# Hybrid-mixer encoder layer on one core: sparse-attention pairs one round behind the local blocks, pooling's scaling on VectorE, pooled products behind the gate turns

## The chip, the cores and the metric

The kernel runs on one core of a Trainium2 chip. The metric is the device time of one execution in microseconds (us), as the median of several runs. Engines are named as in the profile: PE (TensorE; PEld is its weight load), DVE (VectorE), ACT (ScalarE), POOL (GpSimd) and SP (SyncE, which only issues transfers here).

## The reference

One layer of a streaming encoder, 1024 positions by 1024 channels, float32. An adaLN-conditioned RMSNorm feeds one input projection, whose columns go to four token mixers of 256 channels each; their outputs are normalised, concatenated and projected; a gated MLP with a causal depthwise convolution follows, and a final norm.

```python
ya = gmlp_mixer(za, ws, bs)            # spatial gating over blocks of 128 positions
yb = dsa_mixer(q, k, v, qi, ki, wi)    # top-256 keys of a ReLU indexer, then softmax attention
yc = pool_mixer(zc, w, scale)          # below
yd = swa_mixer(q, k, v, sinks)         # window of 128 positions with sinks
x = x + g1 * (rms(concat(ya, yb, yc, yd)) * mix_out_g @ w_out)
x = x + g2 * conv_glu(h, w_up, conv_w, conv_b, w_down)
```

The pooling mixer: for each of four groups of 64 channels with window 2, 4, 8 or 16, the trailing sum of the window over `min(count, window)`, minus the input itself, times a 64x64 matrix per group, times a scale per channel. The change touches how it is computed and when, and the order of the two attentions.

## The kernel before, in words

Positions are split in 8 blocks of 128 (NBLK) and two halves of 4 blocks (HB). Every large product is exact to float32 by splitting each operand in a high and a low part: three matmuls of 128x512 for each 128x128 weight tile. ACT makes the high part of a weight unit (`hi`), POOL the low part (`lo`, line 584), DVE helps at the start. Each engine works through its own list in order and waits on semaphores; the lists are written out by hand and nothing reorders them.

**Input units.** 19 units of 128 columns (N_IN) are projected one after another; ACT moves each out of PSUM (`evac`). Beside them PE computes the indexer's products (`dot`), ACT their ReLU, DVE sums them to scores (`accumulate`). DVE then finds the keys of blocks 2 and 3 by rounds of maximum and replace (`early_round`, lines 1476 and 1482), 32 rounds in all, and starts a bisection for blocks 4 to 7 (`search`, a generator whose pieces `search_for(us)` takes until their nominal lengths fill the budget; each trial counts keys, line 1387). POOL multiplies the adaLN weights by the condition (`ada_products`, line 615), ACT sums them (`ada_sums`).

**Pooling.** Units 9 and 10 (U_C) are the pooling input `zc[0]`, `zc[1]`, each 128 channels of two windows. POOL builds the window sums in `win_a` and `win_b` by doubling (`doubled`, line 591): for `zc[0]` behind unit 14, for `zc[1]` behind units 17 and 18. ACT scales them by one over the window (`pool_scale`, line 826), for `zc[1]` only after all eight gate evacuations. POOL then corrects the first 16 positions (line 597) and subtracts the input (`pool_out`, line 598), and signals `pool_ready`. PE multiplies by the pooling weights in two halves of four blocks (`pooled`, line 2048), into banks 0 and 1 both times, and DVE scales the results into `y` (`pool_outputs`, line 1564).

**The mixers.** After the last input unit PE transposes the gating input block by block (`gate_turn`, line 2004), ACT copies it out (`gate_inputs`, line 938). Then a loop over k interleaves, on PE, DVE and ACT, the local (window) attention of block k with the pairs of sparse-attention heads of the first half. There are 8 pairs (PAIRS), two heads each, two pairs to a block, and pair d runs in round k = d + BEHIND with BEHIND = 2, so the loop has NBLK + BEHIND + 1 = 11 rounds, the first of which has no earlier work to carry and the last ones only sparse work. In round k:

- PE: `swa_values(k-1)` (line 2034), `swa_turn(k, 0)`, `values(d-1, 1)`, `turn(d, 0)`, `swa_turn(k, 1)`, `logits(d+2)` (line 2087), `turn(d, 1)`, `swa_logits(k+2)` (line 2013), `values(d, 0)`; in rounds 0 and 1 also `pooled(k)`.
- DVE: `swa_softmax(k+1)` (lines 1542 to 1548), `soft(k+1-BEHIND)` (line 1612), `swa_out(k-1)`, and spread over the rounds the gMLP statistics (`ln_mean` line 1527, `ln_var` line 1532), the masks of blocks 2 and 3 (`mask_of`, line 1490), `early_out`, the adaLN values (line 1716, round 3), `gmlp_scale` (round 6) and `gmlp_output` (round 8).
- ACT: the exponentials and copies of both attentions.
- POOL: centring and squaring of the gMLP input (lines 686, 689), then the low part of unit 20, then the sum of bias and mask (`masked_bias`, line 670) that `soft(4)` to `soft(7)` need.

Then PE turns `y` (line 2169, 64 small matmuls), and the output projection and the MLP follow with PE always busy. DVE goes on with the bisection beside them: `columns_beside_search` takes pieces between output columns. Its result is needed when the second half's sparse attention starts.

```python
def link(eng, s, ins):       # vlink on DVE, plink on POOL
    ins.then_inc(s, 1)
    eng.wait_ge(s, chain[s.name])
```

## Time and profile before

| what | value |
| --- | --- |
| median of 3 runs | 1263.75 us (1262.98 to 1265.56) |
| the profiled execution's own time | 1264.89 us |
| its span | 1262.9 us |
| PE busy | 1210.7 us, 96% |
| DVE busy | 716.9 us, 57% |
| ACT busy | 580.1 us, 46% |
| POOL busy | 615.1 us, 49% |
| share of PE in the chain that ended last | 86% |
| mean granted clock of PE | 0.985 |

The chain of waits is the way back from the last instruction, at each step to what released it. An engine can be busy all along and yet not be on it. The windows view gives the busy time of each engine in a stretch; a timeline row gives the start of a group of equal instructions, their busy time together and, in brackets, how long the engine had been idle and who ended that. "issue" there is time without a visible reason. Between about 365 us and the end PE is busy without a break but for a few joints, so what matters for the change lies before.

### The profile page before, as it was taken

What the parts mean: (1) busy time and instruction counts of PE and PEld (TensorE: products, weight loads), DVE (VectorE), ACT (ScalarE), POOL (GpSimd) and SP (SyncE); (2) the same over time, 40 slices, a digit from 0 to 9 for tenths busy, and PEclk for the clock granted to TensorE, in tenths of its full rate; (3) what the DMA queues carried; (4) which work ended last, traced back from release to release, by engine and by line L of the source; (5) the groups of instructions that cost most, each with busy time, mean ns of one, the idle gap of its engine ahead of it and who ended that gap; (6) DMA issues with size and microseconds to landing.
All of it is one profiled execution on the core that took longest, in us unless ns stands there. A gap on an engine that the chain in (4) does not pass through costs nothing.

```text
span 1262.9 us, 17256 instructions
## 1 busy us (share of the span) xinstructions
PE 1210.7 (96%) x5814; PEld 1003.5 (79%) x5814; DVE 716.9 (57%) x1412; ACT 580.1 (46%) x997; POOL 615.1 (49%) x309
## 2 busy tenths in 40 slices
PE   6898999987899999999999999999999999999997
PEld 5687788866788888888888887888888888888876
DVE  5953777896968798999983334353522211121233
ACT  5245566645843444134423666552544134422443
POOL 0045756783414255445545666434355445544555
PEclk8899999997999999999999999999999999999999
DMA  8557563450122122232224442424222222222223
GB/s 309 190 186 262 173 204 107 171 150 18 51 84 104 63 100 99 89 112 100 100 100 142 134 142 103 164 76 155 70 100 100 99 87 97 100 100 100 88 106 139
DMA packets 58665, 153.93 MB, mean 122 GB/s; under 512 B 6600, under 2 KB 20296, under 8 KB 58608
## 3 DMA queue, kind: packets, MB, share of 16 engines
q1 hardware_dynamic: 47760, 135.64, 31.2%
q10 hardware_dynamic: 10848, 17.57, 4.3%
q8 instruction: 31, 0.51, 0.2%
q14 instruction: 26, 0.21, 0.1%
HBM read 142.66 MB, written 10.52 MB: 121 GB/s over the span
## 4 chain that ended last, share of the span: by engine, by line
PE 86%; DVE 4%; ACT 4%; DMA 2%; POOL 2%; issue 1%; ACTq 0%; SPq 0%; DVEq 0%; POOLq 0%
PE ps L1938 24%; PE ps L1941 24%; PE ps L1939 24%; PE ps L2229 2%; PE ps L1917 1%; DMA x_sb<-in_x 1%; PE ps L1918 1%; PE ps L1962 1%; PE ps L2218 1%; PE ps L2208 1%; PE ps L1922 1%; PE ps L1864 1%; POOL w_ada L615 1%; PE ps L2242 1%; DMA qi_dram<-qi_lo 1%
## 5 line engine op out<-in xcount | busy, mean ns | idle before, releaser
L575 POOL TENSOR_TENSOR w_lo<-w_raw,w_hi 128x1024 fp32r<-128x1024 f32 x148 | 354.8, 2398 | 436.9 <-ACT w_hi L757 436.9
L1938 PE MATMUL ps<-h_hi,w_hi 128*128 128x512 f32 x896 | 355.4, 397 | 2.6 <-POOL w_lo L584 2.6
L1939 PE MATMUL ps<-h_lo,w_hi 128*128 128x512 f32 x896 | 350.4, 391 | 0.0
L1941 PE MATMUL ps<-h_hi,w_lo 128*128 128x512 f32 x896 | 331.7, 391 | 0.0
L757 ACT ACTIVATE w_hi<-w_raw 128x1024 fp32r<-128x1024 f32 x148 | 156.8, 1059 | 329.6 <-PE ps L1941 322.3
L1938 PEld LDWEIGHTS ps<-h_hi,w_hi 128*128 128x128 f32 x896 | 168.9, 189 | 37.6 <-POOL w_lo L584 3.4
L1941 PEld LDWEIGHTS ps<-h_hi,w_lo 128*128 128x128 f32 x896 | 168.5, 188 | 35.9
L1939 PEld LDWEIGHTS ps<-h_lo,w_hi 128*128 128x128 f32 x896 | 169.2, 189 | 32.7
L1797 DVE SCALAR_TENSOR_TENSOR ps<-conv_in,conv_w,ps 128x512 f32<-128x512 f32 x44 | 33.2, 754 | 205.4 <-ACT ps L1170 205.4
L1938 PE MATMUL ps<-act_hi,w_hi 128*128 128x512 f32 x352 | 139.7, 397 | 2.2 <-DVE act_lo L1738 2.2
L1941 PE MATMUL ps<-act_hi,w_lo 128*128 128x512 f32 x352 | 137.4, 390 | 0.0
L1939 PE MATMUL ps<-act_lo,w_hi 128*128 128x512 f32 x352 | 137.2, 390 | 0.0
L1387 DVE TENSOR_SCALAR_CACHE_REDUCE unread<-score,trial 128x640 uint8<-128x640 f32 (+1 forms) x124 | 130.2, 1076 | 2.2
L1744 DVE SCALAR_TENSOR_TENSOR x<-ps,mod,x 128x512 f32<-128x512 f32 (+1 forms) x64 | 48.0, 749 | 135.8 <-PE ps L1941 135.7
L615 POOL TENSOR_TENSOR w_ada<-w_ada,cond 128x1024 f32<-128x1024 f32 x32 | 76.6, 2405 | 45.5 <-DMA w_ada<-in_w_ada 45.3
L1938 PEld LDWEIGHTS ps<-act_hi,w_hi 128*128 128x128 f32 x352 | 66.2, 188 | 15.9 <-DVE act_lo L1738 2.8
L1941 PEld LDWEIGHTS ps<-act_hi,w_lo 128*128 128x128 f32 x352 | 66.1, 188 | 14.0
L1939 PEld LDWEIGHTS ps<-act_lo,w_hi 128*128 128x128 f32 x352 | 66.2, 188 | 12.7
L1370 DVE SCALAR_TENSOR_TENSOR score<-ps,wis,score 128x512 f32<-128x512 f32 (+3 forms) x70 | 46.0, 657 | 29.3 <-ACT ps L817 25.7
L1177 ACT ACTIVATE conv_t<-ps 128x512 f32<-128x512 f32 x44 | 26.3, 598 | 70.6 <-DVE ps L1801 70.5
L817 ACT ACTIVATE ps<-ps 128x512 f32<-128x512 f32 (+3 forms) x80 | 38.8, 501 | 33.9 <-PE ps L1962 33.8
L1938 PE MATMUL ps<-y_hi,w_hi 128*128 128x512 f32 x128 | 50.1, 392 | 0.0
(264 smaller groups left out, 1856.7 us busy)
## 6 DMA issues: line engine op xcount, KB each, us to landing
w_raw<-in_w SPq DMA_DIRECT2D x173, 512.0 KB, 3.2
w_ada<-in_w_ada SPq DMA_DIRECT2D x48, 512.0 KB, 4.3
x_sb<-in_x SPq DMA_DIRECT2D x4, 1024.0 KB, 9.6
q_st<-qk_dram SPq DMA_DIRECT2D x32, 128.0 KB, 4.3
out<-fin_o ACTq DMA_DIRECT2D x14, 256.0 KB, 2.1
qi_st<-qi_dram ACTq DMA_DIRECT2D x18, 128.0 KB, 4.5
qk_dram<-qk_hi ACTq DMA_DIRECT2D x4, 512.0 KB, 2.7
qk_dram<-qk_lo ACTq DMA_DIRECT2D x4, 512.0 KB, 3.7
```

Source lines behind the costliest of these rows:

```text
L575: pool.tensor_tensor(r(w_lo[:, slot]), w_raw[:, slot], w_hi[:, slot], ALU.subtract).then_inc(w_lo_ready, 1)
L615: pool.tensor_tensor(t, t, cond[:], ALU.mult).then_inc(ada_weighted, 1)
L757: act.activation(r(w_hi[:, slot]), w_raw[:, slot], ACT.Copy).then_inc(w_hi_ready, 1)
L817: act.activation(ps[:, 4 + i % 4, 0:n], ps[:, 4 + i % 4, 0:n], ACT.Relu, scale=IDX_DIM ** -0.5).then_inc(relu_ready, 1)
L1177: act.activation(conv_t[:, u], ps[:, u], ACT.Gelu_apprx_tanh).then_inc(gelu_ready, 1)
L1370: dve.scalar_tensor_tensor(out=dst, in0=ps[:, 4 + i % 4, 0:n], scalar=wgt, in1=dst, op0=ALU.mult, op1=ALU.add).then_inc(scores_added, 1)
L1387: dve.tensor_scalar(unread[:, b % 2, 0:P * (b + 1)], sc_of(b), limit, None, op, ALU.add, accum_out=found[:, b - HB:b - HB + 1]).then_inc(k ...
L1744: dve.scalar_tensor_tensor(out=o, in0=ps[:, bank], scalar=gate, in1=o, op0=ALU.mult, op1=ALU.add).then_inc(residual_added, 1)
L1797: dve.scalar_tensor_tensor(out=ps[:, u], in0=conv_in[:, u, 1:HALF + 1], scalar=conv_w[:, w_row, 1:2], in1=ps[:, u], op0=ALU.mult, op1=ALU. ...
L1938: pe.matmul(ps[:, bank], r(hi_t[:, kk]), r(xh(kk)), start=(i == 0), stop=False)
L1939: pe.matmul(ps[:, bank], r(hi_t[:, kk]), r(xl(kk)), start=False, stop=False)
L1941: mm = pe.matmul(ps[:, bank], r(lo_t[:, kk]), r(xh(kk)), start=False, stop=last_k)
```

## The change

- `BEHIND` is 1: pair d runs in round d + 1, and the loop has 10 rounds. `logits(0)` is issued ahead of the loop. `ada_sums(18)` on ACT goes from round 1 to round 0.
- Pooling: `pool_scale` on ACT and `pool_out` on POOL go away. DVE does both in `pool_mix`: two instructions for each window, one for the first 16 positions and one that scales and subtracts. `pool_mix(0)` stands behind the first 25 top-8 rounds, `pool_mix(1)` behind the two masks, which come ahead of the mixers too.
- The bisection gets 6.0 in place of 9.0 twice before the mixers, and 4.2 in place of 3.6 beside the MLP's columns.
- PE's pooled products of block b come directly behind `gate_turn(b)`, the second half in banks 6 and 7. The first of them waits for both `pool_mix`. DVE's `pool_outputs`, second half first, both come in round 0 behind all the means, and `swa_turn(0, 0)`, which writes bank 6, waits for the first.

```diff
-        BEHIND = 2
+        BEHIND = 1
...
+        POOL_BANKS = ((0, 1), (6, 7))
...
                 elif n == U_POOL + 2:
-                    pool.wait_ge(pool_scaled, 2)
-                    pool_out(0, 0, win_a)
-                    pool_out(0, 64, win_b)
-                elif n == U_POOL + 3:
+                    pool.wait_ge(pool_mixed, 2)
                     doubled(zc[1], 1, win_a, 0)
                     doubled(win_a, 2, win_b, 0)
-                elif n == U_POOL + 4:
+                elif n == U_POOL + 3:
                     doubled(win_b, 4, win_a, 0)
                     doubled(win_a, 8, win_b, 64)
                     pool.sem_inc(pool_summed, 1)
             ada_products(N_IN - 1)
-            pool.wait_ge(pool_scaled, 4)
-            pool_out(1, 0, win_a)
-            pool_out(1, 64, win_b)
-            pool.sem_inc(pool_ready, 1)
...
             gate_inputs(6)
             gate_inputs(7)
-            act.wait_ge(pool_summed, 2)
-            pool_scale(0, win_a, 8)
-            pool_scale(64, win_b, 16)
...
-                        if k == 1:
+                        if k == 0:
                             ada_sums(N_IN - 1)
...
+            def pool_mix(tile, wins):
+
+                dve.wait_ge(pool_summed, tile + 1)
+                for row, sums, win in zip((0, 64), (win_a, win_b), wins):
+                    rows = slice(row, row + 64)
+                    vlink(dve.scalar_tensor_tensor(out=sums[rows, 16:32], in0=sums[rows, 16:32], scalar=float(win),
+                                                   in1=pool_c[rows, tile], op0=ALU.mult, op1=ALU.mult))
+                    dve.scalar_tensor_tensor(out=zc[tile][rows, 16:], in0=sums[rows, 16:], scalar=1.0 / win,
+                                             in1=zc[tile][rows, 16:], op0=ALU.mult, op1=ALU.subtract).then_inc(pool_mixed, 1)
...
+                if step == DOT_STEPS:
+                    pool_mix(0, (2, 4))
                 if taken == ROUNDS and step + 1 < TOP_STEPS:
-                    search_for(9.0)
+                    search_for(6.0)
+            dve.wait_ge(top8_marked, ROUNDS + DROP_ROUNDS)
+            for b in EARLY:
+                mask_of(b)
+            dve.sem_inc(masks_ready, 1)
+            pool_mix(1, (8, 16))
...
                         if k == 0:
-                            ln_mean(2)
-                            ln_mean(3)
-                        if k == 1:
+                            for b in range(2, NBLK):
+                                ln_mean(b)
+                            pool_outputs(1)
                             pool_outputs(0)
...
-                        columns_beside_search(nd, 5 * KD, 0, 3.6)
+                        columns_beside_search(nd, 5 * KD, 0, 4.2)
...
+                if (b, j) == (0, 0):
+                    pe.wait_ge(pool_out_ready, 1)
...
             for b in range(NBLK):
                 gate_turn(b)
+                pooled(b)
...
                 if h == 0:
+                    logits(0)
                     for k in range(NBLK + BEHIND + 1):
...
-                        if k < 2:
-                            pooled(k)
```

PE's list from the first gate turn on, before (za_t is the gating input, dk and dq the local attention's keys and queries, zc the pooling input):

```order
L2004 MATMUL ps<-ident,za_t 128x128 [waits unit_out]
L2004 MATMUL ps<-ident,za_t 128x128 x7
L2004 MATMUL ps<-ident,za_t 128x128 [waits gm_out]
L2004 MATMUL ps<-ident,za_t 128x128 x3
L2004 MATMUL ps<-ident,za_t 128x128 [waits gm_out]
L2004 MATMUL ps<-ident,za_t 128x128 x3
L2013 MATMUL ps<-dk,dq 128x256 [waits swa_biased]
L2013 MATMUL ps<-dk,dq 128x256 x3
L2004 MATMUL ps<-ident,za_t 128x128 [waits gm_out]
```

and with the change, where the product of block 0 stands between the turns of blocks 0 and 1, with a wait of its own:

```order
L1986 MATMUL ps<-ident,za_t 128x128 [waits unit_out]
L1986 MATMUL ps<-ident,za_t 128x128 x3
L2029 MATMUL ps<-pool_w,zc_97 128x128 [waits pool_w_loaded,pool_mixed]
L2029 MATMUL ps<-pool_w,zc_98 128x128
L1986 MATMUL ps<-ident,za_t 128x128 x4
L2029 MATMUL ps<-pool_w,zc_97 128x128
L2029 MATMUL ps<-pool_w,zc_98 128x128
L1986 MATMUL ps<-ident,za_t 128x128 [waits gm_out]
L1986 MATMUL ps<-ident,za_t 128x128 x3
L2029 MATMUL ps<-pool_w,zc_97 128x128
```

Seven turns have moved behind that wait.

DVE's list at the end of the input units, before (score and unread belong to the bisection, swa_bias to the local attention):

```order
L1413 TENSOR_SCALAR trial<-ps 128x2 [waits bound_ready]
L1387 TENSOR_SCALAR unread_126,ps<-score,trial 128x640 [waits trial_set]
L1513 TENSOR_SCALAR kept<-ps 128x8 [waits keys_counted]
L1515 MEMSET swa_bias_in 128x4x64 [waits swa_table_loaded,dve_chain]
L1516 MEMSET swa_bias_in 64x4x64 [waits dve_chain]
L1517 MEMSET swa_bias_in 64x4x64 [waits dve_chain]
L1519 COPY swa_bias<-swa_bias_in 128x1024 [waits unit_done,dve_chain]
L1542 COPY logit<-sinks 128x4 [waits swa_logits_ready,dve_chain]
L1543 SCALAR_TENSOR_TENSOR logit<-ps,swa_bias 128x4x128
```

and with the change, from the third and last trial on:

```order
L1396 TENSOR_TENSOR ps<-ps,wanted 128x2 [waits keys_counted]
L1398 COPY_PREDICATED ps<-ps,trial 128x2 [waits trial_judged]
L1465 TENSOR_SCALAR score<-score 128x384 [waits top8_marked]
L1465 TENSOR_SCALAR score<-score 128x512 [waits dve_chain]
L1472 SCALAR_TENSOR_TENSOR win_a<-win_a,pool_c 64x16 [waits dve_chain,pool_summed]
L1474 SCALAR_TENSOR_TENSOR zc_98<-win_a,zc_98 64x1024 [waits dve_chain]
L1472 SCALAR_TENSOR_TENSOR win_b<-win_b,pool_c 64x16
L1474 SCALAR_TENSOR_TENSOR zc_98<-win_b,zc_98 64x1024 [waits dve_chain]
L1505 TENSOR_SCALAR kept<-ps 128x8 [waits keys_counted]
L1507 MEMSET swa_bias_in 128x4x64 [waits swa_table_loaded,dve_chain]
L1508 MEMSET swa_bias_in 64x4x64 [waits dve_chain]
L1509 MEMSET swa_bias_in 64x4x64 [waits dve_chain]
L1511 COPY swa_bias<-swa_bias_in 128x1024 [waits unit_done,dve_chain]
```

Two masks and the four instructions of `pool_mix(1)` now stand between the bisection and the local attention's table.

DVE's list behind the third pair of `ln_var`, round 3, before (mod and scale_g are the adaLN values, logit_69 the sparse attention's logits, bias its unmasked table, bias_e POOL's sum of bias and mask):

```order
L1716 TENSOR_TENSOR mod<-ada,b_ada 128x32 [waits ada_rest_summed]
L1717 TENSOR_SCALAR scale_g<-mod 128x8 [waits dve_chain]
L1718 TENSOR_TENSOR scale_g<-scale_g,norm_g 128x8 [waits dve_chain]
L1542 COPY logit<-sinks 128x4 [waits swa_turned,swa_logits_ready]
L1543 SCALAR_TENSOR_TENSOR logit<-ps,swa_bias 128x4x256
L1547 TENSOR_REDUCE sm_max_s<-logit 128x4 [waits swa_biased]
L1548 TENSOR_SCALAR sm_neg_s<-sm_max_s 128x4 [waits dve_chain]
L1612 SCALAR_TENSOR_TENSOR logit_69<-ps,bias_68 128x256 [waits dsa_turned,dsa_logits_ready] x2
L1620 TENSOR_REDUCE sm_max<-logit_69 128x1 [waits dsa_biased]
```

and with the change:

```order
L1698 TENSOR_TENSOR mod<-ada,b_ada 128x32 [waits ada_rest_summed]
L1699 TENSOR_SCALAR scale_g<-mod 128x8 [waits dve_chain]
L1700 TENSOR_TENSOR scale_g<-scale_g,norm_g 128x8 [waits dve_chain]
L1534 COPY logit<-sinks 128x4 [waits swa_turned,swa_logits_ready]
L1535 SCALAR_TENSOR_TENSOR logit<-ps,swa_bias 128x4x256
L1539 TENSOR_REDUCE sm_max_s<-logit 128x4 [waits swa_biased]
L1540 TENSOR_SCALAR sm_neg_s<-sm_max_s 128x4 [waits dve_chain]
L1603 SCALAR_TENSOR_TENSOR logit_69<-ps,bias_e 128x384 [waits bias_and_mask,dsa_turned,dsa_logits_ready] x2
L1611 TENSOR_REDUCE sm_max<-logit_69 128x1 [waits dsa_biased]
```

The first pair that needs POOL's `bias_e` follows these `ln_var` one round sooner.

## Rows read from the trace of the kernel before

**Rows 1.** The windows view of the opening (busy us and instructions by engine, clock, DMA share).
```profile
285.00:290.00 5.00, 3.42 (x14) 2.44 (x14) 1.40 (x4) 2.77 (x11) 4.65 (x4) 0.50 0.00 0
```

**Rows 2.** PE's timeline: start us, busy us, group [idle before <-releaser].
```profile
286.93 2.08 PE L2013 MATMUL ps<-dk,dq 64*128 64x256 f32 x8
...
293.88 1.00 PE L2034 MATMUL ps<-dv,swa_pt 128*128 128x64 f32 x8
...
300.01 1.90 PE L2034 MATMUL ps<-dv,swa_pt 128*128 128x64 f32 x16
...
311.02 1.95 PE L2034 MATMUL ps<-dv,swa_pt 128*128 128x64 f32 x16
...
316.90 1.95 PE L2034 MATMUL ps<-dv,swa_pt 128*128 128x64 f32 x16
...
323.19 1.13 PE L2013 MATMUL ps<-dk,dq 64*128 64x256 f32 x8
...
324.75 1.95 PE L2034 MATMUL ps<-dv,swa_pt 128*128 128x64 f32 x16
...
346.83 1.90 PE L2034 MATMUL ps<-dv,swa_pt 128*128 128x64 f32 x16
...
358.12 7.36 PE L2169 MATMUL ps<-diag_y,y 128*128 128x128 f32 x64
```

**Rows 3.** The chain that ended last, in the opening: start us, us, what.
```profile
283.05 0.67 ACT win_a L826
...
285.41 2.36 POOL zc L598
288.14 2.35 POOL zc L598
```

**Rows 4.** DVE's timeline from the last top-8 rounds to the first pooled outputs.
```profile
227.45 0.69 DVE L1476 MAX8 top<-score 128x8 f32<-128x512 f32 x1
...
248.80 0.69 DVE L1476 MAX8 top<-score 128x8 f32<-128x512 f32 x1
...
256.70 0.16 DVE L1413 TENSOR_SCALAR trial<-ps 128x2 int32<-128x2 int32 x1
...
259.21 0.16 DVE L1413 TENSOR_SCALAR trial<-ps 128x2 int32<-128x2 int32 x1
...
270.45 0.17 DVE L1513 TENSOR_SCALAR kept<-ps 128x8 int32<-128x8 int32 x1
...
272.67 2.22 DVE L1519 COPY swa_bias<-swa_bias_in 128x1024 f32<-128x1024 f32 x1 [0.90 <-PE ps L1941]
...
278.47 0.97 DVE L1548 TENSOR_SCALAR sm_neg_s<-sm_max_s 128x4 f32<-128x4 f32 x1
279.35 0.41 DVE L1527 TENSOR_REDUCE st<-gm 128x4 f32<-128x256 f32 x1
...
294.08 1.29 DVE L1564 TENSOR_TENSOR y<-ps,pool_s 128x512 f32<-128x512 f32 x2 [0.84 <-PE ps L2048]
```

**Rows 5.** The source view of lines 1738 and 1282: ns min/median/max, first and last start.
```profile
L1738 DVE TENSOR_TENSOR act_lo<-act_f,act_hi x6: 2275/2381/2397, 506.0 to 1217.9; 128x512 fp32r<-128x512 f32 x6
...
L1282 DVE SCALAR_TENSOR_TENSOR h_t<-x_sb,scale_g,rms_x x8: 1283/1285/1289, 27.7 to 69.9; 128x1024 f32<-128x1024 f32 x8
```

**Rows 6.** POOL's timeline.
```profile
240.83 2.41 POOL L584 TENSOR_TENSOR w_lo<-w_raw,w_hi 128x1024 fp32r<-128x1024 f32 x1
...
316.37 0.61 POOL L686 TENSOR_TENSOR vn<-gm,st 128x256 f32<-128x256 f32 x1 [4.64 <-DVE st L1532]
...
321.25 1.96 POOL L670 TENSOR_TENSOR bias_e<-bias,score 128x384 f32<-128x384 f32 x2
```

**Rows 7.** DVE's timeline in rounds 3 to 5.
```profile
316.47 0.56 DVE L1716 TENSOR_TENSOR mod<-ada,b_ada 128x32 f32<-128x32 f32 x1
...
321.23 0.74 DVE L1612 SCALAR_TENSOR_TENSOR logit<-ps,bias 128x256 f32<-128x256 f32 x2
...
327.34 1.02 DVE L1612 SCALAR_TENSOR_TENSOR logit<-ps,bias_e 128x384 f32<-128x384 f32 x2
```

More of the change, by code:

```diff
@@ L592, in doubled @@
                                          src[row:P, win - 1:16 + S - win], ALU.add))
-            def pool_out(tile, row, sums):
-                rows = slice(row, row + 64)
-                plink(pool.tensor_tensor(sums[rows, 16:32], sums[rows, 16:32], pool_c[rows, tile], ALU.mult))
-                plink(pool.tensor_tensor(zc[tile][rows, 16:], sums[rows, 16:], zc[tile][rows, 16:], ALU.subtract))
             pool.memset(eps[:], EPS).then_inc(consts_set, 1)
@@ L821, in relus @@
                     stack_queries(b + 2)
-            def pool_scale(row, sums, win):
-                rows = slice(row, row + 64)
-                act.activation(sums[rows, 32:], sums[rows, 32:], ACT.Copy, scale=1.0 / win).then_inc(pool_scaled, 1)
             def v_evac(g):
@@ L1587, in _ @@
             ln_mean(1)
-            dve.wait_ge(top8_marked, ROUNDS + DROP_ROUNDS)
             for h in range(2):
@@ L1699, in _ @@
                             swa_out(k - 1)
-                        if k == 1:
-                            pool_outputs(1)
-                        if k >= BEHIND + 2 and k % 2 == 0:
+                        if k >= BEHIND + 2 and (k - BEHIND) % 2 == 0:
                             early_out((k - BEHIND - 2) // 2)
-                        if k < 2:
-                            ln_mean(2 * k + 4)
-                            ln_mean(2 * k + 5)
                         if 1 <= k < 5:
@@ L2037, in swa_values, with pooled @@
                 mm.then_inc(swa_product, 1)
[L2039 to L2041 removed]
+            def pooled(b):
+                if b == 0:
+                    pe.wait_ge(pool_mixed, 4)
                     pe.wait_ge(pool_w_loaded, 16)
[L2043 to L2050 removed]
+                for t in range(2):
+                    at_ = W * (b % 2) + P * t
+                    mm = pe.matmul(ps[:, POOL_BANKS[b // HB][(b // 2) % 2], at_:at_ + P],
+                                   zc[t][:, 16 + P * b:16 + P * b + P], pool_w[:, t], start=True, stop=True)
+                if b % HB == HB - 1:
+                    mm.then_inc(pool_done, 1)
             pe.wait_ge(unit_out, N_IN - 1)
```

27 lines of the change are left out of this document (3 added, 24 removed).

## The prediction

> **What bounds the kernel now.** I read the chain first: PE holds 86% of it, so only PE's idle stretches and its slow ones can be won. The windows put those in one place, between the last input unit (273 us) and the turning of `y` (358.12 us, [rows 2]). In the opening PE works 3.42 of 5 us at half clock, granted 0.50, that is 1.2 in place of 2.4 GHz [rows 1]. Twice as long shows in PE's timeline: eight products of `swa_logits` take 2.08 us there and 1.13 us later [rows 2].
>
> PE's timeline then gives the mixer's rounds by the start of `swa_values`: round 1 at 293.88, round 2 at 300.01, round 3 at 311.02, round 4 at 316.90, round 5 at 324.75, round 8 at 346.83, the turns at 358.12 [rows 2]. So rounds 1 and 2 cost 17.1 us, 3 and 4 13.7 us, 5 to 7 22.1 us, the last three 11.3 us. The chain shows what holds the opening: ACT's two scalings from 283.05, POOL's two subtractions (2.36 and 2.35 us, from 285.41 and 288.14), then PE's pooled products [rows 3].
>
> A third thing is to be seen in DVE's timeline: some short instructions are long. The table copy `swa_bias` takes 2.22 us and `sm_neg_s` on four numbers 0.97 us [rows 4]; in both cases POOL is in the middle of an instruction and DVE ends just after it. `act_lo` = `act_f` - `act_hi`, both inputs in SBUF, 512 elements, takes 2.38 us in the median, each time beside a POOL instruction of 2.4 us [rows 5].
>
> **Part 1, the opening.** It decides the sign of a large term, so it is followed in time.
>
> *pool_mix(0).* The top-8 rounds start at 227.45 and 14 of them take up to 248.80, 1.525 us each [rows 4]. The eighth ends at 239.65. Bare, pool_mix(0) is two large instructions of 1024 elements at 1.28 us (line 1282, two SBUF inputs, [rows 5]) and two of 16 elements, estimated at 0.2: 3.0 us. But POOL runs an adaLN product until 240.83 and `lo` for 2.41 us behind it [rows 6]. By `act_lo` [rows 5] DVE waits out both: 1.2 + 2.4 us. I take 6.5 us, to 246.1. The bounds are 3.0, if such an instruction does not wait, and 9.0 with a third wait.
>
> The Trainium skill (SBUF — State Buffer, Who interferes with whom) says that a VectorE instruction with two SBUF inputs contends with a GpSimd instruction that reads SBUF. By that rule the change puts eight such instructions among POOL's, and the sum is the one below. The trace agrees for `act_lo`; no row shows `scalar_tensor_tensor` on 64 partitions beside POOL.
>
> *Bisection, masks, pool_mix(1).* Seven rounds more end at 256.8. The bisection's first trial came 6.5 us after the rounds and I take 4.3 us, since POOL now waits for a transfer there; then three trials of 2.51 us (256.70 to 259.21, [rows 4]) in place of five and a half: 268.7. The masks are estimated at 0.5 us each, plus a wait of 1.0 and one of 2.4 behind POOL: 273.1. pool_mix(1) with 3.0 us and a wait of 2.4: 278.4. If the order with POOL falls out otherwise, the bisection ends up to 4 us later, but by then POOL has no work left to wait for, so the end moves little.
>
> *First softmax.* Before, `kept` ran at 270.45, and `swa_bias` could start only with the last unit, 272.67 [rows 4]. Now `kept` starts at 278.4, memsets and copy take 2.0, the first softmax 1.7: `sm_neg_s` ends at 282.1, against 279.44 (278.47 + 0.97, [rows 4]). PE waits for `pool_mix` from about 274.5 to 278.4, and the seven gate turns queue behind that.
>
> *To round 1.* DVE: two means, the second softmax 2.7, six means, at 0.53 each (0.41 and a short one behind it, [rows 4]): 289.0. `pool_outputs(1)` 1.3 [rows 4]: 290.3. Only then may `swa_turn(0, 0)` write bank 6. `pool_outputs(0)` and `soft(0)`'s first part give 292.3, `logits(1)` and `swa_logits(2)` 2.7 us at a clock between the levels [rows 2]: round 1 starts at 295.0, against 293.88. **Loss 1.1 us.** ACT's 2.1 us and POOL's 4.9 us of `pool_scale` and `pool_out` are gone from the chain [rows 3], but DVE's lateness and the seven means in one piece eat them. Without any wait for POOL, this is a gain of 3.7.
>
> **Part 2, rounds 1 and 2.** Before, DVE in round 1 waited for each half of the products, and with it the masks and four means stood between; that is why round 2 took 11.0 us. All of it has moved ahead. Round 3 took 5.9 us [rows 2] with larger pairs. I take 5.4 and 5.5: 10.9 in place of 17.1. **Gain 6.2 us**; bounds 3 (a round of 7 us, as rounds 5 to 7 have) and 7.
>
> **Part 3, rounds 3 and 4.** The pairs are one round sooner, the rest stays. POOL's path does not shorten: from the third `ln_var` pair at 316.4, `vn` for two blocks, `lo` of unit 20 and two sums of bias, to 323.2 (321.25 + 1.96, [rows 6]), 6.8 us. DVE's path does: before, it used them at 327.34, 10.9 us after `mod` began at 316.47 [rows 7]. Now `soft(4)` stands where `soft(3)` stood at 321.23 [rows 7], 4.8 us after, of which 0.9 is a wait for POOL; 3.9 without it. **A new wait** of some 2.3 us on DVE, in which PE stands in front of `logits(5)`, loses its clock and pays about 1.4 us more on what follows (2.08 for 1.13 us, [rows 2]). Rounds 3 and 4 take 17.5 in place of 13.7: **loss 3.8 us**; bounds 0 (POOL in time) and 6.
>
> **Part 4, rounds 5 to 7.** DVE, ACT and PE each have about the same list, the table loads for the gMLP root included: 22.1 us stay 22.1. Here the distances logits, softmax, exponential, turn are the same with `BEHIND` 1 as with 2, so no wait comes from it.
>
> **Part 5, the end.** The tail has lost a round. From round 8's start: PE 1.8 `swa_values`, four pieces of 0.9 for gating and values, two turns 0.9, values of the last two heads 0.9, so 7.2 us; then `early_out` and the reciprocal and first diagonal on DVE, 1.6: 8.8 in place of 11.3. **Gain 2.5 us**; bounds 1 and 3.5.
>
> **Part 6, the search moved behind.** Some 6 us of trials run beside the MLP now. The budget of 4.2 gives DVE the same three pieces per column as 3.6 for the later blocks. The cover is PE's work of over 300 us there, and the search now ends many columns before its result is used. I cost it at nothing; if a column's update came late, PE would lose at most a piece, 1.3 us.
>
> **The sum.** -1.1 + 6.2 - 3.8 + 0 + 2.5 = 3.8 us, rounded to 4. The profiled execution took 1264.9 us (span 1262.9 us), 1.1 above the median of 1263.75; I take the difference off the median: **1259.8 us**.
>
> **Rivals.**
> 1. *No waiting on POOL's port.* If the new instructions run beside POOL at 3.0 us a `pool_mix`, the opening gains 3.7 in place of losing 1.1: gain 8.8, **1255.0 us**. Against it stands `act_lo`; for it, that POOL waits for its transfers in part of the time. If part 3's new wait fails to come too: 12.5, 1251.2.
> 2. *PE's queue behind the first pooled product.* `pooled(0)` waits for `pool_mix(1)`, with seven gate turns, the second local logits and so DVE's means behind it. My slack is negative already. Each further POOL instruction waited out costs 2.4 us on all that follows; from the second on, with part 2 at its low bound, the gain of 4 is gone: 4.0 - 4.8 - 1.5 = -2.3, **1266.0 us**, slower. It decides if pool_mix(1) ends after about 282 us.
> 3. *The rounds are bound by work, not by order.* Then one round fewer gives nothing at the end and rounds 1 and 2 give 3: 4.0 - 3.2 - 2.5 = -1.7, with part 3's loss at half again about zero: **1263.6 us**, no change.
>
> The Trainium skill (Perfetto Trace Analysis, Optimizing Scalar/DVE Operations) advises the other way than this change: where VectorE is saturated, work may go to ScalarE. Only the second rival would follow from it, as DVE is the engine that PE waits for at 278 us; the chance given to it already counts that.
>
> **How the numbers follow.** My sum 0.44, rival 1 0.24, rival 2 0.15, rival 3 0.17. A measurement of this kernel tells about 0.2%, 2.5 us, from no change. The sum's own bounds let a little of its chance fall within that. So: faster 0.70, same 0.16, slower 0.14. The range takes rival 1 and most of rival 3 and the edge of rival 2: 1253.5 to 1264.5.
>
> **What would show it.** `pool_mix(0)` beginning at about 239.7 and lasting over 6 us; large `zc` instructions on DVE of 2 to 3.6 us; `pool_mix(1)` ending near 278; the first `swa_values` near 295, rounds 1 and 2 of 5.4 us; DVE idle before the first `bias_e` instruction, released by POOL; 8.8 us from round 8's `swa_values` to the first turn of `y`, near 354. Wrong if `zc` instructions take 1.3 us (rival 1), if the first `swa_values` comes after 299 (rival 2), or if rounds 1 and 2 take over 14 us (rival 3).

## The result

The changed kernel is slower: 1274.18 us median of 20 executions (1263.64 to 1277.38), against 1265.44 us for the kernel before on the same chips; ratio 1.0047, 95% interval 1.0029 to 1.0065 (the two medians alone would give 1.0069, as more than half of the new times lie in an upper group). The forecast was 1259.8 us, faster; both its sign and its range (1253.5 to 1264.5) were wrong.

The executions of the changed kernel differ more than those of the kernel before, and they differ by TensorE's mean granted clock. Eight of the 20 took 1263.6 to 1266.5 us at a mean clock of 0.980 to 0.985, twelve 1271.4 to 1277.4 us at 0.971 to 0.978. The profiled one (1275.1 us, span 1273.1 us, clock 0.972) is of the upper kind; that of the kernel before (1264.9 us, span 1262.9 us) had 0.985. So the trace shows where the time is in the slower executions, and the experiments have to show which part is always there. No execution of the lower kind was profiled for this kernel.

**The profile after.** The windows from the opening to round 7 (busy us and instructions of PE, PE's weight loads, DVE, ACT, POOL; then clock, DMA share, GB/s):

```profile
270.00:280.00 10.00, 5.89 (x34) 5.11 (x33) 9.20 (x17) 2.43 (x4) 2.19 (x1) 0.71 0.83 207
280.00:290.00 10.00, 7.26 (x55) 6.34 (x54) 7.78 (x23) 5.86 (x15) 2.42 (x4) 0.95 0.01 3
290.00:300.00 10.00, 8.41 (x36) 6.53 (x37) 7.26 (x23) 7.40 (x25) 0.00 (x0) 0.56 0.19 55
300.00:310.00 10.00, 9.76 (x44) 8.36 (x44) 5.73 (x15) 4.42 (x17) 3.98 (x7) 0.50 0.00 1
320.00:330.00 10.00, 6.53 (x36) 4.83 (x35) 6.68 (x13) 5.82 (x20) 6.97 (x7) 0.77 0.16 52
330.00:340.00 10.00, 10.00 (x48) 9.30 (x50) 5.90 (x14) 4.36 (x14) 2.50 (x2) 0.55 0.00 0
```

PE's timeline, with its idle stretches in brackets (L2018 is `swa_values`, the start of a round):

```profile
275.97 1.22 PE L2029 MATMUL ps<-pool_w,zc 128*128 128x128 f32 x4 [3.64 <-DVE zc L1474]
...
290.08 0.41 PE L2008 MATMUL ps<-ident,logit 128*128 128x128 f32 x2 [2.54 <-DVE y L1556]
...
295.03 1.97 PE L2018 MATMUL ps<-dv,swa_pt 128*128 128x64 f32 x8
303.25 3.62 PE L2018 MATMUL ps<-dv,swa_pt 128*128 128x64 f32 x16
312.45 1.95 PE L2018 MATMUL ps<-dv,swa_pt 128*128 128x64 f32 x16
...
325.88 1.65 PE L2070 MATMUL ps<-k_st,q_st 128*128 128x384 f32 x4 [3.31 <-DVE logit L1603]
330.80 3.62 PE L2018 MATMUL ps<-dv,swa_pt 128*128 128x64 f32 x16
...
355.97 1.89 PE L2018 MATMUL ps<-dv,swa_pt 128*128 128x64 f32 x16
...
365.30 9.01 PE L2151 MATMUL ps<-diag_y,y 128*128 128x128 f32 x64 [2.04 <-DVE diag_y L1658]
```

Two things differ from [rows 2]. The waits are longer (3.64, 2.54, 3.31 and 2.04 us), and behind them PE works at 1.2 GHz: `swa_values` of sixteen products takes 3.62 us in rounds 2 and 5 and 1.95 in the others, the turns of `y` 9.01 in place of 7.36. In the windows PE is busy 9.76 of 10 us at 0.50 and 10.00 of 10 at 0.55: there it is no longer waiting, it is slow.

The same steps side by side, from starts in PE's timeline, with three kernels of the experiments below ("two behind" is the change without its one round behind):

| us | before | forecast | after | two behind | after, waits filled | after, POOL's order |
|---|---|---|---|---|---|---|
| first `swa_values` | 293.88 | 295.0 | 295.03 | 295.17 | 294.98 | 296.38 |
| rounds 1, 2 | 17.1 | 10.9 | 17.4 | 13.6 | 14.3 | 13.4 |
| rounds 3, 4 | 13.7 | 17.5 | 18.4 | 13.7 | 16.5 | 14.2 |
| rounds 5 to 7 | 22.1 | 22.1 | 25.2 | 22.1 | 23.2 | 22.2 |
| round 8 to turns of `y` | 11.3 | 8.8 | 9.3 | 11.3 | 9.2 | 9.3 |
| turns to first product of the output projection | 7.1 | not priced | 8.8 | 7.1 | 7.2 | 7.1 |
| from there to the end | 897.7 | as before | 899.0 | 897.5 | 899.1 | 897.6 |

Before to after, the differences are +1.15, +0.3, +4.6, +3.1, -2.0, +1.7 and +1.4: together the 10.2 us between the two spans. Of these the first is no larger than chance: a second profile of the changed kernel, below, has its first `swa_values` at 296.17, 1.1 us after this one.

DVE's timeline holds what the prediction said of the port (`pool_mix(0)`, then `pool_mix(1)`):

```profile
237.53 1.18 DVE L1472 SCALAR_TENSOR_TENSOR win_a<-win_a,pool_c 64x16 f32<-64x16 f32 x1
238.74 1.22 DVE L1474 SCALAR_TENSOR_TENSOR zc<-win_a,zc 64x1024 f32<-64x1024 f32 x1
239.99 2.27 DVE L1472 SCALAR_TENSOR_TENSOR win_b<-win_b,pool_c 64x16 f32<-64x16 f32 x1
242.29 1.22 DVE L1474 SCALAR_TENSOR_TENSOR zc<-win_b,zc 64x1024 f32<-64x1024 f32 x1
...
273.03 0.17 DVE L1472 SCALAR_TENSOR_TENSOR win_a<-win_a,pool_c 64x16 f32<-64x16 f32 x1 [0.16 <-DVE score L1465]
273.24 1.22 DVE L1474 SCALAR_TENSOR_TENSOR zc<-win_a,zc 64x1024 f32<-64x1024 f32 x1
...
279.55 0.17 DVE L1540 TENSOR_SCALAR sm_neg_s<-sm_max_s 128x4 f32<-128x4 f32 x1
```

A 16-element instruction takes 1.18 or 2.27 us where POOL is at work and 0.17 where it is not. Which instruction carries the wait is a matter of the moment. In the second profile of the same program the first large one took it:

```profile
240.17 3.38 DVE L1474 SCALAR_TENSOR_TENSOR zc<-win_a,zc 64x1024 f32<-64x1024 f32 x1
243.58 0.17 DVE L1472 SCALAR_TENSOR_TENSOR win_b<-win_b,pool_c 64x16 f32<-64x16 f32 x1
```

There POOL's `lo` had begun at 240.07, 0.10 us ahead of DVE, and took its usual 2.40 us; so it is, with 3.37 to 3.46 us, in ten of the twelve profiles of kernels with this `pool_mix`. In the first profile DVE began 0.09 us ahead of `lo` and took 1.22 us, and POOL's `lo` took 3.39. The new wait of part 3 is there too, in DVE's and in POOL's timeline:

```profile
324.31 0.56 DVE L1603 SCALAR_TENSOR_TENSOR logit<-ps,bias_e 128x384 f32<-128x384 f32 x1 [1.06 <-POOL bias_e L657]
325.27 0.56 DVE L1603 SCALAR_TENSOR_TENSOR logit<-ps,bias_e 128x384 f32<-128x384 f32 x1 [0.40 <-POOL bias_e L657]
```
```profile
320.87 2.36 POOL L584 TENSOR_TENSOR w_lo<-w_raw,w_hi 128x1024 fp32r<-128x1024 f32 x1
323.18 3.87 POOL L657 TENSOR_TENSOR bias_e<-bias,score 128x384 f32<-128x384 f32 x4
```

### The profile page after: what moved, and what is told of

It reads as the page before. It is cut to its first block, busy times and chain, and to the rows that moved or that the text cites. A ratio compares the mean times of both kernels' runs of the same rounds, so it can differ in the third digit from the quotient of the medians.

```text
span 1273.1 us, 17248 instructions
## 1 busy us (share of the span) xinstructions
PE 1227.2 (96%) x5814; PEld 1019.0 (80%) x5814; DVE 723.1 (57%) x1420; ACT 577.1 (45%) x993; POOL 606.3 (48%) x301
## 4 chain that ended last, share of the span: by engine, by line
PE 82%; DVE 7%; DMA 3%; ACT 3%; POOL 2%; issue 2%; SPq 1%; ACTq 0%; DVEq 0%; POOLq 0%
PE ps L1920 22%; PE ps L1921 22%; PE ps L1923 22%; PE ps L2211 2%; DMA w_ada<-in_w_ada 1%; PE ps L2018 1%; PE ps L1899 1%; PE ps L1900 1%; PE ps L1944 1%; PE ps L2200 1%; PE ps L2190 1%; DVE score L1457 1%; PE ps L1995 1%; PE ps L1904 1%; PE ps L1846 1%
```

## The experiments

Theories: **clock** (behind new idle stretches PE's work runs at half clock, in some executions), **lateness** (the rounds wait for DVE, in all executions) and **order** (one round behind asks for `bias_e` before POOL has it). All times are medians. The experiments ran in four sets, each on a chip of its own, with the kernel before timed beside each (1264.1 to 1265.4 us); across sets the ratios to it are compared.

### The same kernel again, and its waits filled

> The changed kernel once more, unedited, beside the three edits of this call. Clock theory (TensorE's granted clock stays at half speed behind the new idle stretches, in some executions and not in others, and this is the whole loss): again times in two groups, 1263 to 1267 and 1271 to 1278 us, the upper group with a mean granted clock of 0.971 to 0.978, the lower with 0.980 or more. Rival lateness (VectorE is later on the path to the rounds, always, by the port waits and the queue behind the first pooled product): times spread evenly about 1270, not by clock.

Measured: 1268.47 us, 12 executions from 1263.38 to 1276.64. Five lie at 1274.7 to 1276.6 (clock 0.972 to 0.975), five at 1263.4 to 1266.4 (0.982 to 0.985), two between, at 1268.1 and 1268.9 (0.979): spread along the clock rather than in two clean groups. Another profile of the upper kind repeats the waits of the first to a hundredth (3.63, 2.54, 3.31 and 2.05 us, 9.01 for the turns of `y`), though the whole lies about 1.1 us later. With the first 20, 17 of 32 executions have a clock under 0.979; of the kernel before it is 15 of 114. At a clock of 0.982 to 0.985 the changed kernel takes 1264.9 us (12 executions) and the kernel before 1264.8 (63): **at the same clock they are equally fast.** (The mean clock is itself a result of the order, so this tells where the time is, and not what made the clock fall.)

```
+            def hold(count, at_):
+                for _ in range(count):
+                    pe.matmul(at_, ident[:], ident[:], start=True, stop=True)
...
+                if (b, j) == (0, 0):
+                    pe.wait_ge(swa_biased, 2)
+                    hold(16, ps[:, 2, 0:P])
...
+                    hold(26, ps[:, 0, 0:P])
                     pe.wait_ge(pool_mixed, 4)
...
+                    if i == 5:
+                        hold(24, ps[:, 0, 2 * P:3 * P])
```

> The changed kernel with matmuls that nobody reads issued by TensorE where it stood idle: 26 before its wait for pool_mixed, 16 before swa_turn(0, 0), 24 before logits(5). Nothing else moves, and VectorE's instructions stay where they were. Clock theory: granted clock 0.9 to 1.0 from 280 to 340 us, rounds 1 and 2 take 14 us or less in place of 17.4, rounds 5 to 7 22 in place of 25.2, and all executions lie in one group, 1259 to 1266 us. Rival lateness: the rounds wait for VectorE, so a higher clock gives nothing; 1264 to 1277 as without them. Rival order (one round behind makes POOL's bias_e late): the same as rival lateness.

Measured: 1268.2 us (1264.68 to 1271.62), clock 0.982 to 0.988, none of 12 under 0.979; of the unfilled kernel, in the same set, it was five of 12. PE's timeline:

```profile
274.44 5.97 PE L1875 MATMUL ps<-ident 128*128 128x128 f32 x52
...
289.17 3.79 PE L1875 MATMUL ps<-ident 128*128 128x128 f32 x32
...
319.38 5.52 PE L1875 MATMUL ps<-ident 128*128 128x128 f32 x48
```

The clock was 1.00 from 270 to 300 us and 0.83, 1.00, 1.00, 1.00 in the windows behind; the upper group is gone. But each filling matmul leaves two records, so they outlast the waits of 3.64, 2.54 and 3.31 us, and the 1259 to 1266 us expected were missed: the median is that of the unfilled kernel. With 13, 9, 12 and, before the turns of `y`, 8:

> The changed kernel with matmuls that nobody reads, this time no longer than the idle stretches that they fill (in the run with 26, 16 and 24 they took 5.97, 3.79 and 5.52 us, and the waits were 3.64, 2.54 and 3.31): 13 before pooled(0), 9 before swa_turn(0, 0), 12 before logits(5), 8 before the turns of y. Clock theory: granted clock near 1.0 from 276 to 375 us, first swa_values at 295 as in the changed kernel, rounds 1 and 2 13.8 us in place of 17.4, rounds 3 and 4 16 to 17.5, rounds 5 to 7 22, the turns of y 7.4 in place of 9.0; 1261 to 1265 us with a clock of 0.985 or more, and no execution over 1270. Rival: the rounds wait for VectorE and the clock is a companion, not a cause; then the median stays at 1268 to 1274.

Measured: 1265.96 us, 1257.39 to 1270.9, ratio to before 0.9999 (0.9977 to 1.0022). The four fastest (1257.4 to 1261.2) have clocks of 0.987 to 0.991, the rest 0.978 to 0.983; one of 12 is under 0.979, against 17 of 32 without filling. Two lie over the 1270 expected as the limit, and the median over the 1261 to 1265. Filling is work of its own: at 0.982 to 0.985 these kernels take 1269.6 us (six executions, long filling) and 1266.6 (seven, short), over the 1264.9 without. A count by clock flatters them, then; by time it is two of 12 over 1270 us, against 17 of 32. The medians part less clearly: the interval of this ratio overlaps that of the unfilled kernel's second run (1.0026, 1.0 to 1.0053). The profiled one (span 1264.4 us) has DVE's work where the changed kernel has it, the first `swa_values` at 294.98, and is 8.7 us shorter. So the lateness theory falls as an account of the loss, while the expected narrow group did not come: the clock still fell from 290 to 300 us (0.67).

### One round behind alone, and the rest alone

```
-        BEHIND = 2
+        BEHIND = 1
...
-                        if k < 2:
-                            pooled(k)
+                        if k == 0:
+                            pooled(0)
+                            pooled(1)
```

> The kernel before with the pairs one round behind alone (both pooled products and their outputs in round 0); pooling's scaling stays on ScalarE and GpSimd. Prediction's terms: part 5 gains 2.5, part 3 loses 3.8 with a wait of some 2 us on VectorE for bias_e, rounds 1 and 2 gain little as the products' waits remain in them: 1264 to 1269. Clock theory: slower than before only in executions in which the granted clock falls behind the wait of logits(5), by some 3 us. Rival order: 1268 or more in every execution, since the order alone is the loss.

Measured: 1278.38 us (6 executions, 1267.82 to 1285.41), ratio 1.0098 (1.0061 to 1.0134); clock 0.963 to 0.982, five of six under 0.979. DVE waits 1.06 and 0.40 us for `bias_e` here too. The 1264 to 1269 expected were missed, and the clock theory's 3 us of loss by far; the order rival's 1268 or more in every execution came but for one of 1267.8, the only one with a clock of 0.982. The run is not one round behind alone: both pooled products had to move into round 0, and in the profile the opening and rounds 1 and 2 are 5.7 us longer than before.

```
-        BEHIND = 1
+        BEHIND = 2
...
-                    logits(0)
```

> The changed kernel with the pairs two rounds behind again; pooling's scaling on VectorE and the pooled products behind the gate turns stay. Clock theory: the idle stretches of 3.6 and 2.5 us before pooled(0) and swa_turn(0, 0) stay, so does the low clock from 290 to 311 us in many executions, and the one before logits(5) goes: two groups, 1263 to 1266 and 1268 to 1274. Rival order: as fast as before or faster, 1260 to 1265, in one group. Rival lateness: 1266 to 1275 in one group.

Measured: 1262.37 us (1260.28 to 1268.44), ratio 0.9986 (0.9971 to 1.0); one of 12 under 0.979. The idle stretches of 3.65 and 3.45 us in the opening are there, and rounds 5 to 7 take 22.1 us. So the change's two halves have opposite signs: pooling on VectorE with the products behind the gate turns gives 3 us, though the interval reaches no gain, and one round behind costs 13 us without it (the moved products included) and 6 to 12 with it (1268.5 and 1274.2 against 1262.4). The clock theory expected a second group here and did not get it, the order rival's 1260 to 1265 came: these opening waits alone did not part the executions, though rounds 1 and 2 were slow in the first profile behind nearly the same ones. Joined, the two theories read: the order makes the wait in round 4, and the clock behind it makes it dear. That is tried next.

### POOL's order in round 3

```
-                    lo(N_IN + 1)
                     tables_ready(0)
...
                     for I in range(HEADS * 2, FIRST_LATE):
                         masked_bias(I)
+                        if I == HEADS * 2 + 1:
+                            lo(N_IN + 1)
```

> The changed kernel with GpSimd's lo of the input behind the first two sums of mask and bias and not ahead of them. Theory (with the pairs one round behind, VectorE needs bias_e 2.4 us before GpSimd has it, and TensorE loses 3.3 us before logits(5) and then its clock): VectorE's waits of 1.06 and 0.40 us for bias_e go, TensorE's wait before logits(5) falls to 1.5 us or less, rounds 3 and 4 take 15 to 16 us in place of 18.35, and round 5 7 in place of 10.4; median 1262 to 1268. Rival (the round is full of VectorE's own work at that place): the wait before logits(5) stays over 2.5 us, median as the changed kernel.

Measured: 1264.68 us (1259.8 to 1270.24), ratio to before 1.0 (0.9977 to 1.0023); three of 12 under 0.979. In the timelines of POOL, DVE and PE:

```profile
318.34 1.95 POOL L657 TENSOR_TENSOR bias_e<-bias,score 128x384 f32<-128x384 f32 x2
320.26 2.37 POOL L584 TENSOR_TENSOR w_lo<-w_raw,w_hi 128x1024 fp32r<-128x1024 f32 x1
```
```profile
320.24 1.01 DVE L1604 SCALAR_TENSOR_TENSOR logit<-ps,bias_e 128x384 f32<-128x384 f32 x2
```
```profile
321.30 0.97 PE L2071 MATMUL ps<-k_st,q_st 128*128 128x384 f32 x4 [1.36 <-DVE logit L1604]
...
355.55 7.38 PE L2152 MATMUL ps<-diag_y,y 128*128 128x128 f32 x64 [2.04 <-DVE diag_y L1659]
```

One POOL instruction moved behind two others: DVE does not wait, PE waits 1.36 us in place of 3.31, rounds 3 and 4 take 14.2 us in place of 18.4, and round 5 7.4 in place of 10.4. All came as expected or better; the rival (DVE full at that place) falls. Between the two profiles a wait that was 1.95 us longer goes with 7.1 us in rounds 3 to 7 (43.5 against 36.4). That is the price in these two executions and not a mean: this one is of the lower kind (1262.2 us), the other of the upper. How much kind matters is seen in rounds 1 and 2, which the edit does not touch: 13.4 us here and 17.4 there. And the turns of `y` ran at full clock behind the same wait of 2.04 us. By time two of 12 are over 1270 us here, as with filling, against 17 of 32 without the edit.

### The opening's order

```
+                            pool_outputs(1)
+                            pool_outputs(0)
                             for b in range(2, NBLK):
                                 ln_mean(b)
-                            pool_outputs(1)
-                            pool_outputs(0)
```

on the kernel two rounds behind:

> Two rounds behind as before, and in the opening VectorE's pool_outputs(1) and (0) ahead of the six ln_mean. Theory (TensorE's wait of 3.45 us before swa_turn(0, 0) is the queue of means on VectorE): the wait falls to 1.3 us, first swa_values at 293.0 in place of 295.17, 1260 to 1261. Rival (the means only move and are missed later, as softmax(2) or vn come late): first round's gain given back by round 3, 1262 to 1263.

Measured: 1263.8 us (1261.61 to 1265.16). PE's wait before `swa_turn(0, 0)` fell from 3.45 to 1.47 us and the first `swa_values` came at 291.99, 3.2 us sooner. Round 2 then took 9.9 us in place of 6.3 and the gain was gone. The reason is neither theory's:

```profile
300.00:310.00 10.00, 9.44 (x42) 7.93 (x42) 5.79 (x16) 4.25 (x16) 3.48 (x6) 0.50 0.14 40
```

PE was busy 9.44 of 10 us at 0.50, though its largest single wait since 289 us was 1.60 us. The median missed both forecasts.

With all eight gate turns ahead of the first pooled product as well:

```
             for b in range(NBLK):
                 gate_turn(b)
+            for b in range(NBLK):
                 pooled(b)
```

> The same and all eight gate turns ahead of the first pooled product. Theory (prediction's second rival: the gate turns, the second local logits and all behind them queue behind pooled(0), which waits for VectorE's pool_mix(1)): the idle stretch of 3.65 us before pooled(0) falls under 1.5, the last pooled product ends by 284 in place of 287.4, first swa_values at 291 to 292, 1257.5 to 1260. Rival (VectorE sets the opening, whatever TensorE's queue): first swa_values at 293 as with the outputs first alone, 1260 to 1262.

Measured: 1267.04 us (1260.52 to 1269.49), a miss for both; five of 12 under 0.979, so that two rounds behind do not by themselves hold the clock. The wait before `pooled(0)` went, and a longer one came. ACT's timeline, then PE's:

```profile
280.82 0.40 ACT L923 ACTIVATE logit<-logit,sm_neg_s 128x129 f32<-128x129 f32 x1 [3.52 <-DVE sm_neg_s L1540]
...
281.61 1.06 ACT L916 ACTIVATE gm<-ps 128x512 f32<-128x512 f32 x2
```
```profile
282.24 1.97 PE L1986 MATMUL ps<-ident,za_t 128*128 128x128 f32 x8 [5.52 <-ACT gm L916]
```

ACT empties the banks of the gate turns, and its exponentials of the first softmax stand in that queue: it waits 3.52 us for DVE's `sm_neg_s` with gate banks full behind it. The queue that matters is ACT's, not PE's.

Two rounds behind, with the pooled products back in rounds 0 and 1 (banks 0 and 1 for both halves, each half waiting for the other's outputs):

> Of the change only pooling's scaling on VectorE and the masks ahead of it: the pairs two rounds behind, the pooled products in rounds 0 and 1 again as in the kernel before, each half waiting for the outputs of the other. It parts the gain of 3.5 us that rounds 1 and 2 show with the products behind the gate turns (13.6 us in place of 17.1). Theory (that gain is the products' place): rounds 1 and 2 take 16 to 17.5 us again, first swa_values at 293 or earlier, since TensorE's four 3.64 and 3.45 us waits shrink, and the median is 1263.5 to 1266. Rival (the gain is the masks' and means' place, which this kernel keeps): rounds 1 and 2 under 15 us, median 1260 to 1263.

Measured: 1265.93 us (1261.59 to 1273.18). The first `swa_values` comes at 288.45, rounds 1 and 2 take 17.1 us again. So the 3.5 us of those rounds are the products' place, as the theory had it, and in the profiles they are more than paid for by an opening that is 6.7 us later (288.45 against 295.17). This kernel lost that lead in round 3, which ran at half clock behind a wait of 2.93 us and took 9.7 us in place of 5.9; three of its 12 executions are under 0.979.

### The best of each order, with filled waits

Two rounds behind, outputs first, 11 filling matmuls before `pooled(0)`, 4 before `swa_turn(0, 0)` and 6 before `swa_turn(1, 1)`:

> The kernel with two rounds behind and the outputs first, with matmuls that nobody reads in TensorE's waits: 11 before pooled(0), 4 before swa_turn(0, 0), 6 before swa_turn(1, 1). Clock theory (the 3.2 us that the outputs first gained were lost again because round 2 ran at 0.50): granted clock over 0.9 from 290 to 310 us, round 2 6 to 6.5 us in place of 9.9, first GEMM of the MLP at 360 in place of 363.97, mean clock 0.987 or more, 1257 to 1260. Rival (round 2 waits for VectorE or ScalarE, the clock only goes along): 1261 to 1264.

Measured: **1257.63 us** (10 executions, 1256.1 to 1264.78), ratio to before 0.9939 (0.9916 to 0.9963): faster than the kernel before, and so than the changed one (1.0047 and 1.0026). PE's timeline, and the windows:

```profile
275.37 0.71 PE L2041 MATMUL ps<-pool_w,zc 128*128 128x128 f32 x4 [1.23 <-DVE zc L1474]
...
287.94 1.10 PE L2029 MATMUL ps<-dv,swa_pt 128*128 128x64 f32 x8
294.47 2.00 PE L2029 MATMUL ps<-dv,swa_pt 128*128 128x64 f32 x16
300.76 1.95 PE L2029 MATMUL ps<-dv,swa_pt 128*128 128x64 f32 x16
```
```profile
290.00:300.00 10.00, 7.75 (x60) 6.20 (x60) 9.62 (x28) 7.04 (x26) 2.48 (x5) 1.00 0.19 54
300.00:310.00 10.00, 9.08 (x76) 7.71 (x73) 9.20 (x22) 7.34 (x26) 6.12 (x9) 1.00 0.23 60
```

Round 2 takes 6.3 us, as the clock theory had it. The first `swa_values` comes 4.1 us sooner than without filling, of which 1.4 are there at `pooled(0)`; that much is near what two profiles of one program differ by. The clock did not stay up to the end: the window from 310 us has 0.83, and the turns of `y` ran slow although PE's waits in the 20 us ahead of them were 0.83 us at most:

```profile
346.43 0.63 PE L2095 MATMUL ps<-ident,logit 128*128 128x128 f32 x4 [0.83 <-ACT p_t L966]
...
349.38 8.99 PE L2162 MATMUL ps<-diag_y,y 128*128 128x128 f32 x64
```

The same on the kernel one round behind, with POOL's order mended and 8 more before the turns of `y`:

> One round behind, GpSimd's lo behind the first two sums of bias, the outputs first, and the same filling matmuls, with 8 more before the turns of y: the changed kernel with every loss taken away that the runs have shown. Clock theory: mean clock 0.987 or more, 1256 to 1260, as the last rounds keep their gain of 2 us. Rival order (one round behind pays elsewhere what it gains at the end): as fast as the kernel two rounds behind with the same fillers, or slower by 1 to 4.

Measured: 1261.57 us, ratio 0.9971 (0.9953 to 0.999), clock 0.984 to 0.988: slower than two rounds behind by 3.9 us, as the rival had it. Here `soft(0)` belongs to round 0 and stood behind the six means:

```profile
292.06 1.11 PE L2083 MATMUL ps<-k_st,q_st 128*128 128x128 f32 x4 [3.39 <-DVE logit L1604]
```

With the means moved behind `soft(0)`:

> The kernel of the last run with one round behind, with the six ln_mean behind soft(0) and not ahead of it: there TensorE stood 3.39 us before logits(1), whose bank VectorE had not read, and the first swa_values came at 295.12, 7.2 us later than with two rounds behind. Theory (one round behind is paid for by waits on VectorE and GpSimd alone, each of which can be ordered away): first swa_values at 289 to 290, granted clock over 0.9 from 290 to 310, and 1255 to 1258 us. Rival (the six means are then missed by GpSimd and ScalarE, and the pairs stand again at logits(3) or logits(5)): first swa_values at 290, but rounds 1 to 4 3 us or more longer than the 27.9 of the last run, 1259 to 1263.

Measured: 1260.28 us (1256.53 to 1264.45), ratio 0.9957 (0.9934 to 0.9979). The first `swa_values` comes at 288.18; rounds 1 and 2 take 17.6 us, the end of one and the start of the other at half clock (0.69 and 0.80 in the windows from 290), rounds 3 and 4 14.1, the last 9.2. So the rival's figures came (1259 to 1263 us, rounds 1 to 4 over 3 us longer), and the theory's 1255 to 1258 did not; and a new wait did come with the means' move, 1.36 us, but before `logits(2)` and not `logits(3)` or `logits(5)`. Mended, one round behind is a little faster than before, but not shown better than two: its interval overlaps that of 0.9916 to 0.9963.

The control, the kernel before with 6, 7, 6 and 13 filling matmuls in its own waits:

> Control: the kernel before with matmuls that nobody reads in its own waits: 6 before swa_logits(1), 7 before swa_turn(0, 1), 6 before the first pooled products, 13 before logits(2). Theory (what the fillers gave to the changed orders is the clock that these had lost; the kernel before lost less, granted 0.67, 0.82 and 0.86 from 280 to 310 us): 1262 to 1264, a gain of 1 to 3 us, so that most of the 7.3 us by which the filled kernel with two rounds behind beats it is the order. Rival (all of those 7.3 us are the fillers): 1256 to 1259.

Measured: 1263.74 us (1260.02 to 1267.17), ratio 0.9981 (0.9959 to 1.0003), granted clock 1.00 in every window from 270 to 380 us. So filling alone gives 1 to 2 us, if anything, and the same order without filling gave no more (ratio 0.9986); most of the 7.3 us of the best kernel is order that a held clock lets through. The two profiles with the clock at 1.00 up to 310 us show it without the clock: here the first `swa_values` is at 291.58 and rounds 1 and 2 take 16.1 us, with the best kernel 287.94 and 12.8, 7.0 us in all.

## Why the prediction was wrong

**Part 1, the opening: right in its sum, by two errors that cancel.** First `swa_values` at 295.03, forecast 295.0. That agreement is partly luck, as the second profile has 296.17. `pool_mix(0)` took 6.0 us (forecast 6.5) and 6.4 in the second profile, by DVE's waiting while POOL works; it began 2.1 us sooner than worked out. `pool_mix(1)` met no wait and ended at 275.9, not 278.4. These 2.5 us were lost again: gate turns and pooled products took PE from 275.97 to 286.6, DVE waited 1.87 us for the second local logits in the middle of them, a wait that the prediction had not, and its six means stood ahead of the outputs. On the port, the trace agrees with the rule that the prediction quoted from the Trainium skill (SBUF — State Buffer, Who interferes with whom): two SBUF inputs beside POOL, 1.18 and 2.27 us in place of 0.17, and 3.38 in place of 1.22.

**Part 2, rounds 1 and 2: the step that failed most.** "I take 5.4 and 5.5" from round 3 of the kernel before. The order gave 3.5 us (13.6 in place of 17.1, two rounds behind), near the low bound of 3, for the rounds took 7.3 and 6.3 us; the other 3.8 us were work at half clock, in the profiled execution of after. The changed kernel's own order, with POOL's edit that lies behind these rounds, took 13.4 when the clock did not stay down. PE is 9.76 of 10 us busy there, so no term made of waits could hold it.

**Part 3, rounds 3 and 4: right.** The wait for `bias_e` came where forecast, and 4.6 us against 3.8. DVE itself waited 1.46 us and not "some 2.3" (the prediction's own 6.8 and 3.9 leave 2.9); PE's wait grew from 1.32 to 3.31 us, and the rest is slow work behind it. The move of one POOL instruction takes it away.

**Part 4, rounds 5 to 7: "22.1 us stay 22.1" was wrong by 3.1.** The wait before `logits(5)` stands at the end of part 3, but its price goes on behind it: round 5 took 10.4 us. The prediction had "loses its clock and pays about 1.4 us more" for eight products; `swa_values` alone, 3.62 for 1.95, adds 1.7, and all of round 5 is slow. The mechanism was seen, its length was not.

**Part 5, the end: gain 2.0 for 2.5**, the same in every kernel one round behind. With the last round gone, PE waits 2.04 us for `diag_y` (within the 9.3). Not priced was that the turns of `y` then ran slow, 1.7 us more. That this comes of the wait is not shown: behind the same wait they took 7.38 us in one run, and with no wait over 0.83 us 8.99 in another. **Part 6** was right: no column waits; the 1.4 us behind the first product appear also in executions of other orders (899.1, 899.0), with a clock of 0.98 in the window from 700 to 800 us.

**The rivals.** None had the mechanism. The second named the right sign and its condition (`pool_mix(1)` after 282) was not met: 275.9. The third was near the order's own effect: rounds 1 and 2 gave 3.5 for its 3, but the end gave 2.0 where it had nothing. The second's own sum takes 1.5 us for part 2 at its low bound, where 6.2 less 3 is 3.2, so that its time should have been 1267.8 and not 1266.0. The first was half true, `pool_mix(1)` met no wait and the opening gained nothing by it. Two of the signs of being wrong would have misled: in the first profile all four large `zc` instructions took 1.22 us though the wait for POOL was there, and rounds 1 and 2 took over 14 us by the clock, not because they were full of work.

What decides: the sum of the prediction has terms for order, and for a fallen clock only the 1.4 us of part 3 and a share of 2.7 us in part 1. The step that failed is that it let parts 2, 4 and 5 run at full clock behind the waits of parts 1 and 3: 10.9 us for rounds 1 and 2 were 17.4, of which 3.8 by half clock, rounds 5 to 7 cost 3.1 us more, and the turns of `y` 1.7. At equal clock the changed kernel and the one before take 1264.9 and 1264.8 us; what it gains at the end and in rounds 1 and 2 is eaten by the wait of round 4 (rounds 3 and 4 take 16.5 us for 13.7 even with the waits filled) and, in these profiles, the opening. The loss of the median is that 17 of 32 executions fall to a clock under 0.979, against 15 of 114.

That the idle stretches bring this about is shown by filling them on the same order: none of 12 executions and one of 12 fell under 0.979, the first beside five of 12 of the unfilled kernel on the same chip. The filled medians are no proof, since filling costs time of its own. Taking the longest wait away gave three of 12 by clock and two of 12 by time, which points the same way and is few. Open is why the same program falls in one execution and not in the next, and how large each wait's part is, as no lower execution of the changed kernel was profiled. The Trainium skill (TensorE: Matmul & The Clock Gate, What's actually happening) says that the number of matmuls that run at the low clock, at the start of a kernel, varies from run to run of the same kernel; by that rule one program has several times, and the trace agrees so far as 0.971 and 0.985 are both here, but no run shows what it varies with. Also not tried was a version in which PE has real work, and not filling, in the opening's waits.

## What to carry over

Price an idle stretch of PE by two numbers: the wait, and the work behind it should the clock fall; in the two profiles compared here 2 us of the first went with 5 of the second. Where a change puts a new wait into a dense stretch, look at the spread of its times and their clocks, not at one profile: in this case two profiles of one program differed by 1.1 us in the opening and showed a port wait on different instructions. Compare at equal clock first. And when a chain is shortened by one step, follow every queue that it passes: here the answer was one POOL instruction of 2.4 us, in a program of 1265.

## What the runs showed of the hardware

- One program, unchanged, ran with a mean granted clock from 0.971 to 0.985 and times from 1263.4 to 1277.4 us; what made them differ is not on record.
- A single wait's length does not tell whether the clock falls: behind 2.04 us before the turns of `y` they took 9.01 us in one kernel and 7.38 in another, with no wait over 0.83 us in the 20 us ahead of them 8.99 in a third, and with no wait over 1.60 us since 289 us a window ran at 0.50.
- Two instructions with SBUF inputs on DVE and POOL that met held each other up, the later one waiting: DVE's 64x1024 took 3.38 us when POOL's `lo` had begun 0.10 us before it, and 1.22 when DVE had begun 0.09 us before `lo`, which then took 3.39 in place of 2.40. Even a 64x16 instruction took 2.27 us in place of 0.17.
- A matmul of 128x128 in f32 leaves two records of 0.115 us each at full clock: 26 of them took 5.97 us.
